# Two-block transformer on one core: local attention placed between tiles of the delta mixer's projection

## The chip, the cores and the metric

The kernel runs on one core of a Trainium2 chip (trn2). Its metric is the time of one launch in microseconds on the device; the median of three runs is given. One execution was also profiled. The core has TensorE (PE, matrix products), VectorE (DVE), ScalarE (ACT), GpSimd (POOL) and SyncE (SP), which here issues the weight loads. Each engine works through its own list of instructions in the order in which they are written; semaphores make one wait for another.

## The reference

Two blocks of two layers each run on 256 tokens of width 1024; the first block puts 16 meta tokens in front. All arithmetic is fp32. The change touches the first layer only. Its mixer projects the 272 normed tokens once and splits the result into a delta part and a window part:

```
proj = u @ w_in        # 272 x 1024 by 1024 x 2832
qa, ka, va, za, ba, aa, qb, kb, vb = split_cols(proj, AB_SIZES)
ya = delta_mixer(qa, ka, va, za, ba, aa, conv_w, a_log, dt_bias, a_out_g)
qb = rmsnorm(qb, bq_g) * (B_HD ** -0.5)      # 8 heads of 64
kb = rmsnorm(kb, bk_g)                       # 2 key heads of 64
yb = window_mixer(qb, kb, vb, sink)
return jnp.concatenate([ya, yb], axis=-1) @ w_out
```

- The delta mixer passes q, k and v (12 chunks of 128 channels) through a centred convolution of five taps over the tokens and a SiLU, divides q and k by their length for each of four heads of 128, and then solves and scans a gated delta rule in both directions.
- The window mixer is attention with |t - s| <= 128, a penalty on the distance with one slope for each head, a sink logit for each head, and the 16 meta tokens as keys without a penalty.

## The kernel before

**Layout.** Activations are kept transposed, channels on partitions and 272 tokens along the row. Every fp32 product with weights is made of three products of rounded parts: high by high, low by high and high by low. A block of 512 weight columns (2 MB) lands in one of the two halves of `raw`; for each quarter ACT writes the high part `w_hi` (L1140) and DVE the low part `w_lo` (L1615). A tile is 128 output columns: 8 x 3 matmuls of 128x272 at L524 into one of four banks. DVE then reads the bank, multiplies it by the token's norm factor (`scaled`, L1654) and so frees it for the tile after the next three.

**Order.** Weights are used in the order of `weight_plan`: four blocks `ab_qkvz` (16 tiles: q, k, v for the delta mixer, then z), one block `ab_qb` (four tiles, the window's queries), and `ab_kvb` (three tiles: its keys, its values, and the delta mixer's gates). All 23 tiles come first. In between DVE does a convolution after every second tile (`conv_after`: L1927 once, then L1929 four times), and ACT its SiLU (L1357).

**Head norms** (`head_norms`, `norm_steps`). For each unit ACT squares (L1187), PE sums over the partitions with a matrix of ones (L620), ACT takes the logarithm and the exponential that make the inverse root (L1197, L1200), and DVE scales (L1687, or L1970 for the delta heads). The window's five units run alone behind the projection.

**Window attention** (`attention`). It has 24 units: three groups of queries (16 meta tokens, twice 128) by eight heads. The loop's step k does parts of several units on each engine: PE the scores of unit k (L658), the three transposes of the probabilities of unit k-3 (L668) and the three value products of unit k-5 (L680); DVE the biased logits (L1766), their maximum (L1773, L1774), the sum with the sink and its inverse (L1784, L1785), the scaling of the probabilities (L1787) and the low part of a result (L1630); ACT the exponentials (L1235, L1236), the copy of the transposes (L1250) and the high part of a result (L1259). Every third step carries one of the eight delta head norms (`delta_norm`).

**Behind it.** `gated_delta` transposes k and v (L745), sums the decays (L753) and then works chunk by chunk; its first product is L770. The mask products of its inverse are POOL's (L2404). POOL's other work is the sum of squares for the norms (L2378) and some small loads.

## Time and profile before

| | |
|---|---|
| median of three runs | 1775.62 us (1772.45 to 1776.26) |
| the profiled execution: its own time | 1774.72 us |
| its span, first to last instruction | 1772.9 us |
| PE busy | 1669.5 us, 94% of the span |
| PE loading weights (beside its matmuls) | 1563.7 us |
| DVE busy | 1177.6 us, 66% |
| ACT busy | 816.9 us, 46% |
| POOL busy | 139.9 us, 8% |
| mean granted clock of PE | 0.939 |
| chain that ended last | PE 86%, DVE 9%, ACT 2%, issue 2% |

The granted clock is the share of PE's full speed that it was given in a stretch: 1.00 is 2.4 GHz, 0.50 is 1.2 GHz. A matmul's busy time runs from issue to its modelled end and overlaps the next one, so a busy PE need not be a PE at its full rate. The page's line of 40 slices shows where the clock was low; the stretches of the rows below do it in finer steps. The chain of waits is followed back from the last instruction: at each step to what released it.

### The profile page before, as it was taken

Reading aid. Unit: us, or ns where it says so; the run is one execution under the profiler, and the core shown is the slowest. Engines: PE = TensorE matmul, PEld = TensorE weight load, DVE = VectorE, ACT = ScalarE, POOL = GpSimd, SP = SyncE. Lnnn points to the kernel's source line nnn. Section 1 sums busy time; section 2 is a strip of 40 time slices with the busy share of each in tenths; the row PEclk is TensorE's granted clock in tenths of the full one; section 3 lists DMA queues with packets and bytes.
Section 4 is the critical chain, followed back from the end, with each engine's and each line's share of the span. In section 5 each row is a group of like instructions: output and inputs, shape, how many; then the busy total and the mean of one; then the engine's idle time right before and its main releaser. Section 6 shows DMA issues by size and latency. Waiting matters only on the chain.

```text
span 1772.9 us, 32025 instructions
## 1 busy us (share of the span) xinstructions
PE 1669.5 (94%) x12741; PEld 1563.7 (88%) x12741; DVE 1177.6 (66%) x2136; ACT 816.9 (46%) x1454; POOL 139.9 (8%) x142
## 2 busy tenths in 40 slices
PE   7979899899999889999999898999999999899998
PEld 6935688899999769999999587999998989799998
DVE  6865466577777566777766765666676666566766
ACT  4454322254345455444545445544453555554443
POOL 2000043010002101000200020100010001010000
PEclk9955699899999899999999689999999999999999
DMA  6410000145445304555454122455544444255552
GB/s 235 158 48 1 1 1 1 48 144 189 172 160 203 139 1 155 192 181 185 162 204 157 48 96 96 136 198 190 183 161 153 146 143 144 95 161 190 178 188 94
DMA packets 125816, 236.59 MB, mean 133 GB/s; under 512 B 2614, under 2 KB 50025, under 8 KB 125689
## 3 DMA queue, kind: packets, MB, share of 16 engines
q1 hardware_dynamic: 124393, 230.28, 37.5%
q0 software_dynamic: 1296, 4.53, 0.8%
q8 instruction: 90, 1.47, 0.3%
q14 instruction: 37, 0.30, 0.1%
HBM read 233.75 MB, written 1.05 MB: 132 GB/s over the span
## 4 chain that ended last, share of the span: by engine, by line
PE 86%; DVE 9%; ACT 2%; issue 2%; POOL 0%; SPq 0%; DMA 0%; DVEq 0%; ACTq 0%
PE ps L524 46%; PE ps L571 5%; PE ps L570 5%; PE ps L569 5%; PE ps L532 5%; PE ps L680 4%; PE ps L658 4%; DVE w_lo L1615 2%; PE ps L620 2%; PE ps L668 2%; PE ps L791 1%; PE ps L803 1%; PE ps L800 1%; DVE u_lo L1635 1%; DVE hidden L1666 1%
## 5 line engine op out<-in xcount | busy, mean ns | idle before, releaser
L1140 ACT ACTIVATE w_hi<-raw 128x1024 fp32r<-128x1024 f32 x440 | 460.1, 1051 | 301.0 <-PE ps L571 138.6
L1615 DVE TENSOR_TENSOR w_lo<-raw,w_hi 128x1024 fp32r<-128x1024 f32 x440 | 539.6, 1227 | 9.8 <-ACT w_hi L1140 9.6
L524 PE MATMUL ps<-u_hi,w_hi 128*128 128x256 f32 (+1 forms) x1544 | 444.5, 288 | 15.7 <-DVE u_lo L1635 8.7
L524 PE MATMUL ps<-u_hi,w_lo 128*128 128x256 f32 (+1 forms) x1544 | 440.5, 285 | 0.0
L524 PE MATMUL ps<-u_lo,w_hi 128*128 128x256 f32 (+1 forms) x1544 | 440.1, 285 | 0.0
L524 PEld LDWEIGHTS ps<-u_hi,w_hi 128*128 128x128 f32 x1544 | 294.4, 191 | 19.7 <-DVE u_lo L1635 10.8
L524 PEld LDWEIGHTS ps<-u_hi,w_lo 128*128 128x128 f32 x1544 | 294.6, 191 | 0.0
L524 PEld LDWEIGHTS ps<-u_lo,w_hi 128*128 128x128 f32 x1544 | 293.6, 190 | 0.3
L524 PE MATMUL ps<-a_hi,w_hi 128*128 128x256 f32 (+1 forms) x800 | 230.4, 288 | 5.3 <-DVE a_lo L1630 2.3
L524 PE MATMUL ps<-a_lo,w_hi 128*128 128x256 f32 (+1 forms) x800 | 227.7, 285 | 0.0
L524 PE MATMUL ps<-a_hi,w_lo 128*128 128x256 f32 (+1 forms) x800 | 227.5, 284 | 0.0
L569 PE MATMUL ps<-a_hi,w_hi 128*128 128x256 f32 (+1 forms) x688 | 195.1, 284 | 0.8 <-DVE hidden L1666 0.8
L571 PE MATMUL ps<-a_hi,w_lo 128*128 128x256 f32 (+1 forms) x688 | 195.6, 284 | 0.0
L570 PE MATMUL ps<-a_lo,w_hi 128*128 128x256 f32 (+1 forms) x688 | 195.3, 284 | 0.0
L1666 DVE TENSOR_TENSOR hidden<-ps,hidden 128x256 f32<-128x256 f32 (+1 forms) x272 | 116.0, 427 | 117.3 <-PE ps L571 60.2
L524 PEld LDWEIGHTS ps<-a_hi,w_hi 128*128 128x128 f32 x800 | 153.2, 192 | 7.2 <-DVE a_lo L1630 2.8
L1654 DVE TENSOR_TENSOR work<-ps,rs 128x256 f32<-128x256 f32 (+1 forms) x153 | 65.4, 428 | 141.6 <-PE ps L524 120.8
L524 PEld LDWEIGHTS ps<-a_hi,w_lo 128*128 128x128 f32 x800 | 153.6, 192 | 0.0
L524 PEld LDWEIGHTS ps<-a_lo,w_hi 128*128 128x128 f32 x800 | 152.5, 191 | 0.4
L569 PEld LDWEIGHTS ps<-a_hi,w_hi 128*128 128x128 f32 x688 | 129.8, 189 | 1.0 <-DVE w_lo L1615 1.0
L571 PEld LDWEIGHTS ps<-a_hi,w_lo 128*128 128x128 f32 x688 | 130.0, 189 | 0.0
L570 PEld LDWEIGHTS ps<-a_lo,w_hi 128*128 128x128 f32 x688 | 129.3, 188 | 0.0
(338 smaller groups left out, 2497.4 us busy)
## 6 DMA issues: line engine op xcount, KB each, us to landing
raw<-in_w_ff_dram SPq DMA_DIRECT2D x32, 2048.0 KB, 8.4
raw<-in_ffn_w_gu_dram SPq DMA_DIRECT2D x44, 1024.0 KB, 7.0
raw<-in_ffn_w_down_dram SPq DMA_DIRECT2D x10, 2048.0 KB, 7.8
raw<-in_xa_w_kv_dram SPq DMA_DIRECT2D x8, 2048.0 KB, 7.9
raw<-in_od_w_in_dram SPq DMA_DIRECT2D x6, 2048.0 KB, 8.0
raw<-in_w_in_ab_dram SPq DMA_DIRECT2D x5, 2048.0 KB, 8.5
raw<-in_ev_w_in_dram SPq DMA_DIRECT2D x5, 2048.0 KB, 7.8
raw<-in_xa_w_q_dram SPq DMA_DIRECT2D x4, 2048.0 KB, 7.8
```

What stands on the lines that cost most here:

```text
L524: mm = pe.matmul(bank[:, 0:n], wx[:, q, k * P:(k + 1) * P], x[ux][:, k, ts], start=k == 0 and i == 0, stop=k == KD - 1 and i == 2)
L532: mm = pe.matmul(bank[:, at:at + n_quarters * n].rearrange("p (q n) -> p q n", n=n), x[ux][:, k, ts], wx[:, q:q + n_quarters, k * P:k * P ...
L569: pe.matmul(tile_bank[t % 4][:, 0:n], hi[:, k, cols], a[0][:, at_k, ts], start=k == 0, stop=False)
L570: pe.matmul(tile_bank[t % 4][:, 0:n], hi[:, k, cols], a[1][:, at_k, ts], start=False, stop=False)
L571: mm = pe.matmul(tile_bank[t % 4][:, 0:n], lo[:, k, cols], a[0][:, at_k, ts], start=False, stop=k == chunks - 1)
L620: mm = pe.matmul(banks[u_ % 2][:, 0:n], matrix, hn_sq[:, u_ % 2, i * n:(i + 1) * n], start=i == 0, stop=i == tiles - 1)
L658: mm = pe.matmul((b4, b5)[v % 2][0:x["nq"], 0:x["nk"]], q, k, start=c == 0, stop=c == len(x["q"]) - 1)
L680: mm = pe.matmul(tile_bank[1 + v % 3][x["parts"], r * P:r * P + x["nq"]], vs[r], at_pt[0:rows, v % 2, c, 0:x["nq"]], start=c == 0, stop=c ...
L1140: act.activation(quarter(w_hi, b, q), raw_quarter(b, q), ACT.Copy).then_inc(high_split, 1)
L1615: dve.tensor_tensor(quarter(w_lo, b, q), raw_quarter(b, q), quarter(w_hi, b, q).bitcast(F32), ALU.subtract)\
L1654: dve.tensor_tensor(target, tile_bank[t][:, 0:n], rs[:, ts] if scale is None else scale, ALU.mult)\
L1666: dve.tensor_tensor(hidden[:, k, ts], tile_bank[t][:, 0:ts.stop - ts.start], hidden[:, k, ts], ALU.add)\
```

## The change

The window part is computed first, and the rest of the projection lies inside its attention loop.

- **Order of the blocks.** `ab_qb` and `ab_kvb` come before `ab_qkvz`. The five head norms of the window have the three tiles of `ab_kvb` and the first two of `ab_qkvz` between them. The other 14 tiles lie in steps 0 to 13 of the attention loop (`window_step`). A memset clears the quarter of `raw` that the second block does not fill.
- **Units.** The eight units of 16 queries become one of kind "meta": its 128 rows are 8 heads by 16 queries, taken from a copy `q_meta`, with a table for each row's slope and a sink for each row. So there are 17 units. These units have one bank for their transposes and one for their results (`turn_bank`, `attention_bank`), where there were two and three, since the projection holds the four tile banks.
- **Convolutions.** Chunks 2, 5, 8 and 11 stay on DVE, the other eight go to POOL with nine tensor_tensor operations each. ACT applies one Silu to all twelve chunks in step 12, after all convolutions.
- **Delta norms.** Two groups of four heads: one square of 128x1088, four sums into the tile banks, four logarithms, one exponential, one scaling. They lie in steps 13 to 15; the transposes of k and v in steps 16 to 18; the decays in steps 0 to 2.

Line numbers in the changed kernel are larger. 
```diff
-    add("ab_qkvz", [[cols(x, c)] for c in range(0, 2048, BLOCK)])
     add("ab_qb", [[cols(x, 2064)]])
     add("ab_kvb", [[cols(x, 2576, 256), cols(x, 2048, 128, into=256)]])
+    add("ab_qkvz", [[cols(x, c)] for c in range(0, 2048, BLOCK)])
...
+            if x["kind"] == "meta":
+                return b7[:, 0:n * NMETA].rearrange("p (c q) -> p c q", q=NMETA)
+            bank = b7 if near(x) else tile_bank[1 + v % 3]
+            return bank[x["parts"], 0:n * P].rearrange("p (c q) -> p c q", q=P)[:, :, 0:x["nq"]]
+        def near(x):
+            return x["kind"] in ("window", "meta")
+        def turn_bank(x, v):
+            return b6 if near(x) else (b6, b7)[v % 2]
...
-            for m in range(3):
+            for m in (1, 2):
                 for h in range(8):
                     yield m, h
+        WINDOW_UNITS, AB_BEFORE = 17, 2
+        CONV_DVE = (2, 5, 8, 11)
+        conv_part = area(mx, 9952, 2, T)
+        delta_sq, delta_r = area(work, 0, 4, T), area(work, 4 * T, 4, T)
...
         # TensorE, attention()
+                    if near(x):
+                        if v >= 1:
+                            pe.wait_ge(at_copied, v)
+                    elif v >= 2:
...
-            for t in range(3):
+            def kvb_tile(t):
                 split_ready(b, t if t < 2 else 3)
                 bank_free(b, t)
                 transposed_tile(t, u, full, tile_bank[t]).then_inc(tile_summed, 1 if t < 2 else 2)
+            def qkvz_tile(n):
+                tile_t(first_of("ab_qkvz") + n // 4, n % 4, u, full)
+            head_norms([(1, T, blk64)] * 5, between=lambda i: kvb_tile(i) if i < 3 else qkvz_tile(i - 3))
...
+            def window_step(k):
+                if k < 16 - AB_BEFORE:
+                    qkvz_tile(AB_BEFORE + k)
+                if k == 0:
+                    pe.wait_ge(M["ab_turn_read"], 1)
+                if k == 1:
+                    delta_decays()
+                if k == 2:
+                    pe.wait_ge(M["d_cum_read"], 1)
+                j = k - (16 - AB_BEFORE)
+                if j in (0, 1):
+                    if j == 0:
+                        pe.wait_ge(tile_read, tile_at[first_of("ab_out")])
+                    else:
+                        pe.wait_ge(M["d_rs"], 1)
+                    pe.wait_ge(M["d_sq"], j + 1)
+                    for h in range(A_HEADS):
+                        mm = pe.matmul(tile_bank[h][:, 0:T], ones, delta_sq[:, h], start=True, stop=True)
+                    mm.then_inc(M["d_qsum"], 1)
+                if j in (2, 3, 4):
+                    for i in (2 * j - 4, 2 * j - 3):
+                        delta_turn(i, *turn_list[i])
...
         # ScalarE
-            def conv(first_slot):
-                def silu(i, t):
-                    slot = first_slot + 4 * i + t
-                    if slot % 2 == 0 and slot >= 2:
-                        c = slot // 2 - 1
-                        act.wait_ge(M["conv_done"], c + 1)
-                        act.activation(qkv[:, c], qkv[:, c], ACT.Silu).then_inc(M["silu_done"], 1)
-                return silu
...
+            def window_step(k):
+                if k < 15:
+                    split_high(ab + 1 + (k + 1) // 4, (k + 1) % 4)
+                if k == 2:
+                    act.wait_ge(M["d_cum_read"], 1)
+                    act.activation(necc[0:NMETA, 0], gcc[0:NMETA, 0], ACT.Exp)
+                    act.activation(necc[:, 1:3], gcc[:, 1:3], ACT.Exp).then_inc(M["d_gate_exp"], 1)
+                j = k - (16 - AB_BEFORE)
+                if j == -2:
+                    act.wait_ge(M["conv_done"], 12)
+                    act.activation(qkv, qkv, ACT.Silu).then_inc(M["silu_done"], 1)
+                    log_and_exp()
+                if j == -1:
+                    act.wait_ge(M["silu_done"], 1)
+                    act.activation(delta_sq, qkv[:, 0:4], ACT.Square).then_inc(M["d_sq"], 1)
+                if j in (0, 1):
+                    act.wait_ge(M["d_qsum"], j + 1)
+                    if j == 1:
+                        act.wait_ge(M["d_normed"], 1)
+                    for h in range(A_HEADS):
+                        ins = act.activation(delta_r[:, h], tile_bank[h][:, 0:T], ACT.Ln, bias=eps)
+                    link(ins)
+                    act.activation(delta_r, delta_r, ACT.Exp, scale=-0.5).then_inc(M["d_rs"], 1)
+                    if j == 0:
+                        act.activation(delta_sq, qkv[:, 4:8], ACT.Square).then_inc(M["d_sq"], 1)
+                if j in (2, 3, 4):
+                    for i in (2 * j - 4, 2 * j - 3):
+                        m, source = turn_list[i]
+                        n = TILES[m][1] - TILES[m][0]
+                        act.wait_ge(M["d_turned"], i + 1)
+                        act.activation((v_tok if source == 8 else k_tok)[0:n, m], tile_bank[i % 4][0:n, 0:4 * P].rearrange(
+                            "p (h d) -> p h d", h=4), ACT.Copy).then_inc(M["d_copied"], 1)
...
         # VectorE
+                lag = 5 if near(units[0]) else 6
+                for k in range(n + lag):
                     if k < n:
                         maximum(k)
                     if 0 <= k - 1 < n:
                         normalise(k - 1)
-                    if k >= 6:
-                        result(k - 6)
                     if between is not None:
                         between(k)
+                    if k >= lag:
+                        result(k - lag)
+                    if after is not None:
+                        after(k)
...
+            def qkvz_step(c):
+                if c == 0:
+                    split_low(ab, 2)
+                scaled(za[:, c - 12] if c >= 12 else xa[:, c, 2:2 + T], c % 4, tile_at[ab] + c, full)
+                split_low(ab + 1 + c // 4, c % 4 - 1)
...
+            def conv_step(k):
+                if k + 1 in CONV_DVE:
+                    conv(k + 1)
...
+                j = k - (16 - AB_BEFORE)
+                if j in (0, 1):
+                    heads = qkv[:, 4 * j:4 * j + 4].rearrange("p h t -> p (h t)")
+                    dve.wait_ge(M["d_rs"], j + 1)
+                    dve.scalar_tensor_tensor(heads, heads, P ** -0.5 if j == 0 else 1.0, delta_r.rearrange("p h t -> p (h t)"),
+                                             ALU.mult, ALU.mult).then_inc(M["d_normed"], 1)
...
         # GpSimd
+            for c in range(12):
+                if c not in CONV_DVE:
+                    weights = [col("conv", 12 * j + c).to_broadcast([P, T]) for j in range(5)]
+                    taps = [xa[:, c, j:j + T] for j in range(5)]
+                    pool.wait_ge(tile_read, tile_at[phases["ab_qkvz"].first] + c + 1)
+                    pool.tensor_tensor(qkv[:, c], taps[0], weights[0], ALU.mult)
+                    link(pool.tensor_tensor(conv_part[:, 1], taps[1], weights[1], ALU.mult))
+                    for j in range(1, 5):
+                        if j < 4:
+                            pool.tensor_tensor(conv_part[:, (j + 1) % 2], taps[j + 1], weights[j + 1], ALU.mult)
+                        ins = pool.tensor_tensor(qkv[:, c], qkv[:, c], conv_part[:, j % 2], ALU.add)
+                        if j < 4:
+                            link(ins)
+                    ins.then_inc(M["conv_done"], 1)
```

DVE around one step of the window loop; `ps` is a bank, `att` the logits and probabilities, `mx` the projection and the convolutions. Before:

```order
L1766 SCALAR_TENSOR_TENSOR att<-early,ps 128x272 [waits at_exp,at_scored]
L1773 TENSOR_REDUCE small<-att 128x1 [waits dve_step]
L1774 TENSOR_SCALAR small<-small 128x1 [waits dve_step]
L1784 TENSOR_TENSOR small<-small 128x1 [waits at_exp]
L1785 RECIPROCAL small<-small 128x1 [waits dve_step]
L1787 TENSOR_SCALAR att<-att,small 128x272 [waits dve_step]
L1630 TENSOR_TENSOR a_lo<-ps,a_hi 64x128 [waits operand_high]
```

The same step in the changed kernel, one of the four that have a convolution on DVE:

```order
L1849 SCALAR_TENSOR_TENSOR att<-early,ps 128x272 [waits at_exp,at_scored]
L1856 TENSOR_REDUCE small<-att 128x1 [waits dve_step]
L1857 TENSOR_SCALAR small<-small 128x1 [waits dve_step]
L1867 TENSOR_TENSOR small<-small 128x1 [waits at_exp]
L1868 RECIPROCAL small<-small 128x1 [waits dve_step]
L1870 TENSOR_SCALAR att<-att,small 128x272 [waits dve_step]
L1737 TENSOR_TENSOR mx<-ps,rs 128x272 [waits tile_summed]
L1698 TENSOR_TENSOR w_lo<-raw,w_hi 128x1024 [waits high_split]
L1713 TENSOR_TENSOR a_lo<-ps,a_hi 64x128 [waits operand_high]
L2014 TENSOR_SCALAR mx<-mx,late 128x272 [waits tile_read]
L2016 SCALAR_TENSOR_TENSOR mx<-mx,late 128x272 [waits dve_step] x4
```

The tile's scaling, the weight split and the convolution have moved in between the scaling of the probabilities and the next unit's logits.

POOL, behind its small loads and ahead of the mask products. Before:

```order
L2383 DMA small<-in_a_log_dram 128x8
L2383 DMA small<-in_dt_bias_dram 128x8
L2383 DMA small<-in_b_sink_dram 128x8
L2383 DMA small<-in_od_w_g_2_dram 128x8x16
L2404 TENSOR_TENSOR work<-work,early 16x64 [waits d_nn]
```

In the changed kernel, the first convolution of eight alike:

```order
L2481 DMA small<-in_od_w_g_2_dram 128x8x16
L2502 TENSOR_TENSOR mx<-mx,late 128x272 [waits tile_read]
L2503 TENSOR_TENSOR mx<-mx,late 128x272
L2506 TENSOR_TENSOR mx<-mx,late 128x272 [waits pool_step]
L2507 TENSOR_TENSOR mx<-mx 128x272
L2506 TENSOR_TENSOR mx<-mx,late 128x272 [waits pool_step]
L2507 TENSOR_TENSOR mx<-mx 128x272
L2506 TENSOR_TENSOR mx<-mx,late 128x272 [waits pool_step]
L2507 TENSOR_TENSOR mx<-mx 128x272
L2507 TENSOR_TENSOR mx<-mx 128x272 [waits pool_step]
```

72 operations stand where there were none, each convolution behind a wait for its tile.

ACT where it does the SiLU of the convolutions, in the change at steps 12 and 13 of the loop; `w_hi` is a quarter of weights, `work` the squares. Before, at the end of the projection:

```order
L1140 ACTIVATE w_hi<-raw 128x1024 [waits tile_summed]
L1357 ACTIVATE mx<-mx 128x272 [waits conv_done]
L1140 ACTIVATE w_hi<-raw 128x1024 [waits tile_summed] x2
L1357 ACTIVATE mx<-mx 128x272 [waits conv_done]
L1339 ACT_TABLE_LOAD
```

In the changed kernel:

```order
L1309 ACTIVATE att,small<-att,small 128x272
L1213 ACTIVATE w_hi<-raw 128x1024 [waits tile_summed]
L1457 ACT_TABLE_LOAD
L1457 ACTIVATE mx<-mx 128x3264 [waits conv_done]
L1412 ACT_TABLE_LOAD
L1323 ACTIVATE att<-ps 16x128 [waits at_summed,at_turned]
L1323 ACTIVATE att<-ps 128x256
L1332 ACTIVATE a_hi<-ps 64x128 [waits at_summed]
L1308 ACTIVATE small<-small 128x1 [waits at_prob,at_turned,at_max]
L1309 ACTIVATE att,small<-att,small 128x272
L1213 ACTIVATE w_hi<-raw 128x1024 [waits tile_summed]
L1461 ACTIVATE work<-mx 128x1088 [waits silu_done]
```

Twelve Silu operations and their table load have moved from the projection into the loop as one, which waits for the last convolution; copies, results and exponentials of the next steps stand behind it.

## Rows read from the trace of the kernel before

**Rows 1.** Busy time by stretch; the first row names the columns.
```profile
core 0: us, PE busy (x) PEld busy (x) DVE busy (x) ACT busy (x) POOL busy (x), PEclk, DMA share, GB/s
22.30:92.60 70.30, 68.44 (x540) 67.87 (x538) 59.59 (x109) 30.10 (x38) 0.00 (x0) 1.00 0.49 162
113.00:196.20 83.20, 82.85 (x282) 44.62 (x281) 45.31 (x168) 40.93 (x165) 0.00 (x0) 0.50 0.00 1
147.24:183.26 36.02, 36.02 (x106) 18.66 (x106) 18.50 (x66) 16.98 (x63) 0.00 (x0) 0.50 0.00 1
1070.00:1080.00 10.00, 8.34 (x62) 7.90 (x62) 5.30 (x10) 5.53 (x10) 0.00 (x0) 1.00 0.57 197
```

**Rows 2.** Timeline of PE: start, length in us, instruction.
```profile
90.97 0.29 PE L524 MATMUL ps<-u_hi,w_lo 128*128 128x272 f32 x1
...
108.36 1.09 PE L658 MATMUL ps<-mx 64*16 64x272 f32 x4 [3.40 <-issue]
...
201.33 1.06 PE L770 MATMUL ps<-cst,small 16*128 16x16 f32 x8 [0.33 <-DVE small L1992]
```

**Rows 3.** Chain of waits, window attention: start, us, what.
```profile
178.00 1.66 PE ps L680 x6
...
180.87 0.74 PE ps L668 x3
181.60 1.66 PE ps L680 x6
183.26 1.21 PE ps L620 x2
```

**Rows 4.** Chain of waits, the other layer's attention, same columns.
```profile
645.57 1.05 PE ps L680 x6
...
647.41 1.05 PE ps L680 x6
```

**Rows 5.** Groups by line and shape, 112 to 200 us, columns as in the page.
```profile
L1787 DVE TENSOR_SCALAR att<-att,small 128x272 f32<-128x272 f32 x16 | 5.8, 361 | 0.6
...
L1197 ACT ACTIVATE work<-ps,cst 128x272 f32<-128x272 f32 x8 | 3.8, 474 | 0.1
...
L1774 DVE TENSOR_SCALAR small<-small 128x1 f32<-128x1 f32 x16 | 3.4, 214 | 0.6
...
L1784 DVE TENSOR_TENSOR small<-small 128x1 f32<-128x1 f32 x16 | 2.4, 151 | 1.7 <-ACT att L1236 1.7
```

**Rows 6.** The same view, 20 to 95 us.
```profile
L1615 DVE TENSOR_TENSOR w_lo<-raw,w_hi 128x1024 fp32r<-128x1024 f32 x24 | 29.2, 1217 | 0.0
...
L1140 ACT ACTIVATE w_hi<-raw 128x1024 fp32r<-128x1024 f32 x24 | 25.0, 1053 | 14.3 <-PE ps L524 14.1 <-DMA raw<-in_w_in_ab_dram 0.2
...
L1929 DVE SCALAR_TENSOR_TENSOR mx<-mx,late 128x272 f32<-128x272 f32 x46 | 23.1, 502 | 1.6
...
L1654 DVE TENSOR_TENSOR mx<-ps,rs 128x272 f32<-128x272 f32 x21 | 9.2, 438 | 3.9 <-PE ps L524 3.6 <-DVE mx L1918 0.3
...
L1927 DVE TENSOR_SCALAR mx<-mx,late 128x272 f32<-128x272 f32 x12 | 4.2, 353 | 0.0
...
L1357 ACT ACT_TABLE_LOAD x1 | 1.3, 1283 | 0.0
```

**Rows 7.** Timeline of POOL, delta mixer: start, length in us.
```profile
225.94 1.26 POOL L2404 TENSOR_TENSOR work<-early 128x512 f32<-128x512 f32 x1 [1.13 <-DVE mx L2031]
227.16 1.71 POOL L2404 TENSOR_TENSOR work<-work,early 128x512 f32<-128x512 f32 x1
```

**Rows 8.** Timeline of DVE, the same moments.
```profile
225.97 1.78 DVE L2022 TENSOR_TENSOR mx<-mx 128x512 f32<-128x512 f32 x1
227.67 1.23 DVE L2021 COPY small<-att 128x4 f32<-128x4 f32 x1
228.93 0.69 DVE L2022 TENSOR_TENSOR att<-att,mx 128x512 f32<-128x512 f32 x1
```

**Rows 9.** POOL's line L2378, whole trace: shortest, median, longest in ns.
```profile
L2378 POOL TENSOR_TENSOR square_sum<-square_sum,squares x77: 719/1192/1772, 11.0 to 1575.4; 128x256 f32<-128x256 f32 x56, 128x272 f32<-128x272 f32 x21
```

More of the change, by code:

```diff
@@ L991, in _ @@
+            attention(units, None, between=window_step)
             window_ready = op[0]
@@ L1751, in _, with attention @@
             at = [0]
-            def attention(units, between=None):
+            def attention(units, between=None, after=None):
                 base, n = at[0], len(units)
@@ L1891, in mlp_swiglu @@
                 down(b, ts, norm)
+            dve.memset(raw[:, 1, :, 3 * P:4 * P], 0.0)
             dve.wait_ge(turned, 1)
@@ L1973, in _ @@
[L1973 to L1977 removed]
+            link(dve.tensor_tensor(sink_of, table("meta_head"), sink, ALU.mult))
+            dve.tensor_reduce(sink_meta, sink_of, AX.X, ALU.add).then_inc(M["sink_meta"], 1)
```

234 lines of the change are left out of this document (116 added, 118 removed).

## Prediction, made before the changed kernel was run

> **What bounds the kernel now.** I read the stretches by time first, then PE's timeline at the stage borders, then the chain of waits, and only then the groups by line. From 22.3 to 92.6 us PE works through the first layer's input projection: 68.4 us busy out of 70.3, granted clock 1.00 [rows 1]. Its 540 matmuls in 70.3 us make 3.1 us for a tile of 24. The last projection matmul starts at 90.97 us, the first window score at 108.36 us [rows 2]: 17 us in which DVE and ACT work off the projection's tail and the five norms of the window's heads. From 113 to 196.2 us PE is busy 82.85 of 83.2 us, but at granted clock 0.50 [rows 1]. So the window attention is bound by PE at 1.2 GHz: one unit of 128 queries takes 181.60 - 178.00 = 3.60 us, and every third one carries a norm sum of 1.21 us [rows 3]. A unit of much the same work in the other layer, at the full clock, takes 647.41 - 645.57 = 1.84 us [rows 4]. The delta mixer's own algebra begins at 201.33 us [rows 2]. All the change's work lies before that point; what comes behind it (1772.9 - 201.3 = 1571.6 us) keeps its instructions. I therefore work out one number: when L770's first matmul starts in the changed kernel.
>
> **Up to step 0.** The projection now begins with the window's five blocks' worth: nine tiles (four of qb, three of kvb, two of qkvz) stand ahead of the attention instead of 23, and the five head norms lie between them. 91.3 less 14 tiles of 3.1 us is 47.9 us; five sums at half of 1.21 us add 3.0; six small transposes, the doubling of the keys and the new copy of the meta queries (ACT, a few operations of some 0.4 us) end at about 54 us. That is step 0 of the attention. The 17 us gap is gone, because PE has tiles while ACT and DVE do the norms. The 24 units become 17: the eight with 16 queries go, one "meta" unit comes.
>
> **One step of the new loop.** Steps 0 to 11 each hold an attention unit and a tile; the last convolution must be done in step 12, since ACT then waits for all twelve before its one Silu. Per step:
> - PE: 1.84 + 3.1 = 4.9 us at the full clock.
> - ACT: 16.98 us for nine units [rows 1] is 1.9, with the old delta norms in it, plus 1.05 for a quarter of weights [rows 6]: 2.9 us. Never the bound here.
> - DVE: 18.50 us for nine units is 2.06, less a third of the old norm scaling, an operation like L1654's 0.44: 1.9. To this come the split w_lo 1.22, the scaled tile 0.44, and one convolution in three steps, (0.353 + 4 x 0.502) / 3 = 0.79 [rows 6]. Together 4.4 us, just under PE.
> - POOL: eight convolutions of nine operations of 128x272. The nearest row has 719 ns as its shortest [rows 9]; a following one starts 0.04 us before that (1.26 long, 1.22 apart) [rows 7], so 0.68 x 72 = 49 us, or 4.1 us a step.
>
> By these figures alone PE would set the step at 4.9 us. But DVE and POOL do not run beside each other freely. POOL works from 225.94 to 227.16 and DVE's L2022, which reads two SBUF operands and starts at 225.97, takes 1.78 us; the same operation with POOL quiet takes 0.69 [rows 7, 8]. POOL's next then takes 1.71 instead of 1.26, and behind it a DVE copy of four columns takes 1.23. They take turns, each waiting for the other's whole instruction. The Trainium skill ("SBUF — State Buffer", section "SBUF: two separate sides") says the same as a rule that speaks against this change: the port pair that the two share is locked for a whole instruction, by DVE operations with two SBUF inputs or in a two-port mode, and the loser blocks. By this rule the step is the sum of both engines' locked time, without it 4.9 us; the trace agrees with the rule.
>
> What DVE locks per step: w_lo 1.22, convolution 0.79, the probabilities' scaling 0.36, and the two tiny ones 0.21 and 0.15 [rows 5, 6] (the four-column copy waited too, so I count them): 2.7 us. The score bias, tile scaling and result split read PSUM and one SBUF operand; I count them free. 4.1 + 2.7 = 6.8 us. **I take 6.8 us a step.** Lower end: no turn-taking at all, 4.9 us. Upper end: each of the 5.7 locking instructions of a step waits a whole POOL operation, 4.4 + 5.7 x 0.68 = 8.2 us. If DVE ran ahead of POOL, ACT would wait for POOL in step 12 instead, so the sum stays.
>
> PE is then busy 4.9 of 6.8 us, 72%. A stretch of tiles mixed with head norms with 83% busy keeps clock 1.00 (the last row) [rows 1]; a dense attention of this kind keeps 0.50. I assume some cold spells, hidden in PE's 1.9 us of slack.
>
> **Behind step 12.** The tail has few tiles and much latency. From ACT's step 12: attention part 1.5, split 1.05, two table loads of 1.28 and a Silu of 3264 columns, three times L1140's 1.05: 8.3 us. Step 13: 2.5 and a square of 1.1. Step 14: PE's four norm sums, cold 4 x 1.21 = 4.8 us, four logarithms of 0.47 and an exponential of 1.1, the second square 1.1: 8.9. Step 15: sums 4.8, logarithms and exponential 3.0: 7.8. By then 28.6 us. Step 16 waits for this, then two turns of four transposes at 0.25 us each (three took 0.74) [rows 3] and copies: 3.5. Steps 17 and 18: transposes and values 2.4, turns 2, waiting for copies: 4.8 each. Steps 19 to 21 (transposes, values, twelve small matmuls of the meta unit, each behind the copy and the split of the one before, because there is now one bank for turns and one for results): 2.4, 1.7, 2.3. Sum 48 us; all warm some 42, with more waits 54. The decays, their cumulative sums and the transposes of k and v, which came behind the attention before, are in it or hidden in steps 0 to 2. The wait added on ACT in step 12 has the copies, results and exponentials of steps 13 on queued behind it, and with these PE's scores; that is why the steps are counted in series.
>
> **Sum.** L770 starts at 54 + 12 x 6.8 + 48 = 183.6 us instead of 201.3: 17.7 us less. The profiled execution took 1774.72 us, span 1772.9, which stands 0.9 below the median of 1775.62. 1774.7 - 17.7 = 1757.0, against the median 1758.
>
> What else is priced at nothing: the first weights (the same 2 MB block), the memset of raw on DVE (the quarter it clears belongs to the second block, which PE reads long after), the small table loads on POOL's queue, which stand ahead of its convolutions as before; the delta mask operations behind them start only after 183 us, POOL being free by about 136.
>
> **Rivals.**
> - *A, the forecast*: DVE and POOL take turns, 6.8 us a step: 1758. Chance 0.48.
> - *B, PE bound*: the turn-taking costs little, because POOL lags in harmless gaps. 54 + 12 x 4.9 + 48 = 160.8, 40.5 us less: 1735. For it: DVE's many PSUM operations, in which POOL can work. Against it: what DVE and POOL did to each other [rows 7, 8]. Chance 0.22.
> - *C, every lock waits in full*: 7.8 to 8.2 us a step, L770 at 195.6 to 200.4: 1770 to 1775. For it: POOL has always an operation queued, so the next begins the moment DVE lets go; POOL's mean under load is well above its shortest. Chance 0.18.
> - *D, slower*: the clock. If PE falls to 1.2 GHz as in the old window stage and stays, a step is 3.60 + 6.2 = 9.8 us: 54 + 117.6 + 48 = 219.6, 18.3 us more: 1794. It decides from (201.3 - 102) / 12 = 8.3 us a step, i.e. if PE is cold for about 70% of the loop. For it: PE stayed at 0.50 for 83 us while busy 99.6%. Against it: each step has 24 dense matmuls of the kind that kept 1.00. Chance 0.10. The Trainium skill ("TensorE: Matmul & The Clock Gate", "Part 4: PE-mode transpose") says that transposes don't count as activity in the way matmuls do, which would leave the attention's part weaker still; the other layer's units with their three transposes each held the full clock [rows 4], so the trace bears it out at most in part.
> - *E, it doesn't do what it says*: weights, misc loads or the meta unit's inputs are late and the loop starts late, about 0 to 5 us less than before: 1772. Chance 0.02.
>
> **How the numbers follow.** Time 1758. The range takes in A, B and the better part of C: 1734 to 1773. Changes under 0.2% (3.6 us) can't be told from none here. Faster: A, B and three quarters of C, 0.84; same: the rest of C and part of E, 0.06; slower: D, 0.10.
>
> **What would show it.** After the change: PE's granted clock near 1.00 from 54 to 135 us; DVE's w_lo at a mean of 1.5 to 1.9 us instead of 1.22 in this stretch, and the convolutions' scalar_tensor_tensor near 1.1 instead of 0.50; POOL's 128x272 operations over 0.8 us; step distance of the scores 6.8 us; the first score near 53; the Silu on ACT at about 138; L770 at 184. Wrong it is if DVE's durations stay as they are (B), if the step is 8 us or more (C, D), or if ACT's tail is not in the chain.

## The result, and the profile after

The changed kernel takes 1744.06 us (median of four runs, 1737.77 to 1746.24), beside 1774.03 for the kernel before (median of four, 1770.53 to 1776.26). The ratio is 0.9827 with a 95% interval of 0.9801 to 0.9854: some 30 us less, where 17.7 were forecast. The profiled execution took 1741.96 us, span 1739.6, so 33.3 us less than the span before. PE is busy 1633.7 us (94%), DVE 1158.7 (67%), POOL 202.2 (12%); PE's mean granted clock is 0.962 instead of 0.939.

In the changed kernel the tile's matmuls are L546, scores L685, transposes L698, values L724; `w_lo` is L1698, the tile's scaling L1737, the result's low part L1713; DVE's convolutions are L2014 and L2016, POOL's L2502 to L2507; the first delta product is L796. In some experiments an edit shifts these lines by two (L798, L726, L1851).

The first view is the timeline of PE in the changed kernel: start, length in us, instruction, and in brackets the idle time before it with what ended it.

```profile
68.29 0.72 PE L685 MATMUL ps<-mx 64*128 64x272 f32 x2 [2.14 <-DVE small L2076]
...
81.78 0.29 PE L546 MATMUL ps<-u_lo,w_hi 128*128 128x272 f32 x1
...
83.25 0.72 PE L685 MATMUL ps<-mx 64*128 64x272 f32 x2
83.91 0.49 PE L698 MATMUL ps<-cst,att 128*16 128x128 f32 x3
87.19 1.70 PE L724 MATMUL ps<-att,mx 16*64 16x128 f32 x6 [2.79 <-DVE a_lo L1713]
94.22 0.72 PE L685 MATMUL ps<-mx 64*128 64x272 f32 x2
...
137.10 2.10 PE L1034 MATMUL ps<-work,cst 128*128 128x272 f32 x8 [0.90 <-DVE mx L1737]
139.13 0.72 PE L685 MATMUL ps<-mx 64*128 64x272 f32 x2
...
165.33 1.03 PE L796 MATMUL ps<-cst,small 16*128 16x16 f32 x4
```

The first score starts at 53.31 us and the delta mixer's algebra at 165.33, where it was 201.33 [rows 2]: 36.0 us earlier. The sixteen scores of 128 queries start at 53.31, 57.18, 62.21, 68.29, 73.91, 78.01, 83.25, 94.22, 99.46, 104.70, 110.64, 115.88, 121.12, 128.88, 134.12 and 139.13. The first twelve steps take 67.8 us, 5.65 each. Six of the fifteen steps are exactly 5.24, which is PE's own work at the full clock (the first experiment shows it). The first five have less to do, because the transposes and values of the units lag behind the scores: in the first experiment, where PE never waits, they take 3.87 to 5.03. Two steps are long: 10.97 (from the seventh score) and 7.76 (from the thirteenth). A smaller stop lies early: the fourth score waits 2.14 us for DVE's copy of the decays (L2076), and the step behind it takes 5.62.

The same kernel by stretch, columns as in [rows 1]:

```profile
57.00:121.00 64.00, 58.41 (x369) 48.72 (x368) 56.60 (x120) 25.33 (x72) 57.50 (x67) 0.92 0.25 88
...
85.00:90.00 5.00, 2.81 (x11) 2.18 (x12) 4.86 (x12) 1.86 (x5) 4.84 (x6) 0.69 0.01 3
90.00:95.00 5.00, 5.00 (x25) 4.49 (x24) 0.79 (x3) 1.58 (x4) 4.77 (x7) 0.62 0.00 0
...
52.40:121.25 68.85, 63.26 (x400) 52.77 (x400) 61.35 (x132) 28.25 (x84) 62.19 (x72) 0.93 0.26 92
...
165.30:1739.60 1574.30, 1496.16 (x11830) 1438.36 (x11829) 1048.97 (x1809) 718.04 (x1194) 130.48 (x125) 0.96 0.40 138
```

In the loop PE, DVE and POOL are each busy nine tenths of the time: three engines of nearly equal load. The clock is 0.92 there, against 0.50 in the window stage before [rows 1]. The first two short stretches are the long step: PE idles, the clock falls, and the next tile runs at half speed (from 88.89 to 94.29, 5.4 us instead of 3.2). The last row is all that follows the delta mixer's start; it was 1571.6 us long before.

Groups by line and shape in the changed kernel, 57 to 121 us, to be held against [rows 5, 6]:

```profile
L2507 POOL TENSOR_TENSOR mx<-mx 128x272 f32<-128x272 f32 x31 | 31.1, 1003 | 0.6
...
L2506 POOL TENSOR_TENSOR mx<-mx,late 128x272 f32<-128x272 f32 x22 | 16.3, 740 | 1.7
L1698 DVE TENSOR_TENSOR w_lo<-raw,w_hi 128x1024 fp32r<-128x1024 f32 x11 | 14.8, 1349 | 0.0
L2016 DVE SCALAR_TENSOR_TENSOR mx<-mx,late 128x272 f32<-128x272 f32 x16 | 13.3, 829 | 0.6
...
L1870 DVE TENSOR_SCALAR att<-att,small 128x272 f32<-128x272 f32 x11 | 5.9, 536 | 0.4
...
L2014 DVE TENSOR_SCALAR mx<-mx,late 128x272 f32<-128x272 f32 x4 | 2.6, 653 | 0.0
L1857 DVE TENSOR_SCALAR small<-small 128x1 f32<-128x1 f32 x11 | 2.4, 214 | 0.4
L1867 DVE TENSOR_TENSOR small<-small 128x1 f32<-128x1 f32 x11 | 2.2, 201 | 0.0
```

`w_lo` costs 1.35 us instead of 1.22, the convolution's four operations 0.83 instead of 0.50, the probabilities' scaling 0.54 instead of 0.36, L2014 0.65 instead of 0.35, L1867 0.20 instead of 0.15; L1857 never waited (214 ns in both). Over a step that is 0.13 + (0.30 + 4 x 0.33) / 3 + 0.18 + 0.05 = 0.90 us.

### The profile page after: what moved, and what is told of

It is laid out like the page before. It is cut to its first block, busy times and chain, and to the rows that moved or that the text cites. A ratio compares the mean times of both kernels' runs of the same rounds, so it can differ in the third digit from the quotient of the medians.

```text
span 1739.6 us, 31776 instructions
## 1 busy us (share of the span) xinstructions
PE 1633.7 (94%) x12684; PEld 1552.0 (89%) x12684; DVE 1158.7 (67%) x2044; ACT 804.9 (46%) x1391; POOL 202.2 (12%) x214
## 3 DMA queue, kind: packets, MB, share of 16 engines
HBM read 233.76 MB, written 1.05 MB: 135 GB/s over the span
## 4 chain that ended last, share of the span: by engine, by line
PE 83%; DVE 11%; issue 3%; ACT 2%; POOL 0%; SPq 0%; DMA 0%; DVEq 0%; ACTq 0%
PE ps L546 45%; PE ps L593 6%; PE ps L592 6%; PE ps L591 6%; PE ps L554 5%; DVE w_lo L1698 3%; PE ps L724 3%; PE ps L685 2%; PE ps L642 2%; PE ps L817 1%; PE ps L829 1%; PE ps L826 1%; PE ps L698 1%; DVE u_lo L1718 1%; DVE hidden L1749 1%
## 5 line engine op out<-in xcount | busy, mean ns | idle before, releaser
L1698 DVE TENSOR_TENSOR w_lo<-raw,w_hi 128x1024 fp32r<-128x1024 f32 x440 | 540.5, 1229 | 11.2 <-ACT w_hi L1213 10.9
L546 PE MATMUL ps<-u_hi,w_hi 128*128 128x256 f32 (+1 forms) x1544 | 448.0, 290 | 15.4 <-DVE u_lo L1718 9.0
L546 PE MATMUL ps<-u_hi,w_lo 128*128 128x256 f32 (+1 forms) x1544 | 442.0, 286 | 0.0
L546 PE MATMUL ps<-u_lo,w_hi 128*128 128x256 f32 (+1 forms) x1544 | 441.8, 286 | 0.0
L546 PEld LDWEIGHTS ps<-u_hi,w_hi 128*128 128x128 f32 x1544 | 296.0, 192 | 22.1 <-DVE u_lo L1718 11.0
L546 PEld LDWEIGHTS ps<-u_hi,w_lo 128*128 128x128 f32 x1544 | 296.1, 192 | 0.0
L546 PEld LDWEIGHTS ps<-u_lo,w_hi 128*128 128x128 f32 x1544 | 294.9, 191 | 0.5
L546 PE MATMUL ps<-a_hi,w_hi 128*128 128x256 f32 (+1 forms) x800 | 230.3, 288 | 5.3 <-DVE a_lo L1713 2.3
L546 PE MATMUL ps<-a_lo,w_hi 128*128 128x256 f32 (+1 forms) x800 | 227.7, 285 | 0.0
L546 PE MATMUL ps<-a_hi,w_lo 128*128 128x256 f32 (+1 forms) x800 | 227.4, 284 | 0.0
L546 PEld LDWEIGHTS ps<-a_hi,w_hi 128*128 128x128 f32 x800 | 153.2, 192 | 7.2 <-DVE a_lo L1713 2.8
L1737 DVE TENSOR_TENSOR work<-ps,rs 128x256 f32<-128x256 f32 (+1 forms) x153 | 65.4, 427 | 139.6 <-PE ps L546 118.8
L546 PEld LDWEIGHTS ps<-a_hi,w_lo 128*128 128x128 f32 x800 | 153.6, 192 | 0.0
L546 PEld LDWEIGHTS ps<-a_lo,w_hi 128*128 128x128 f32 x800 | 152.5, 191 | 0.4
L2473 POOL COPY square_sum<-squares 128x256 f32<-128x256 f32 (+1 forms) x11 | 5.7, 516 | 1112.9 <-ACT squares L1235 1092.3
```

The source lines that it names most:

```text
L546: mm = pe.matmul(bank[:, 0:n], wx[:, q, k * P:(k + 1) * P], x[ux][:, k, ts], start=k == 0 and i == 0, stop=k == KD - 1 and i == 2)
L1698: dve.tensor_tensor(quarter(w_lo, b, q), raw_quarter(b, q), quarter(w_hi, b, q).bitcast(F32), ALU.subtract)\
L1737: dve.tensor_tensor(target, tile_bank[t][:, 0:n], rs[:, ts] if scale is None else scale, ALU.mult)\
```

## Experiments

All ratios are to the kernel before, run on the same chip at the same time. The place to look at is the start of the first delta product, "delta start" below; the whole time scatters more (the changed kernel run again shows by how much).

### One operation of each POOL convolution

```diff
+ins = pool.tensor_tensor(qkv[:, c], taps[0], weights[0], ALU.mult)
-pool.tensor_tensor(qkv[:, c], taps[0], weights[0], ALU.mult)
-link(pool.tensor_tensor(conv_part[:, 1], taps[1], weights[1], ALU.mult))
-...   # the three further products and four sums
```

> The changed kernel, but each of the eight convolutions on POOL is only its first of nine operations (the rest of these convolutions is left out). Theory 1, as the trace of the changed kernel suggests: POOL's operations slow DVE's by about 0.8 us a step, DVE and PE are then level at 5.2 us, and the loop's excess over 12 x 5.24 us (4.9 us) comes from steps in which DVE is late. Without POOL's work DVE has 4.4 us a step, so PE sets 5.2 in every step: the first L796-like matmul comes 5 us earlier, about 160, w_lo back at 1.22 us. Theory 2, the forecast's: turn-taking sets the step in full: 8 us or more earlier. Rival: POOL is beside the path, no change within 1 us.

Measured: 1729.43 us, ratio 0.974 (0.9703 to 0.9778), delta start 154.52. Its groups and its row for 57 to 121 us:

```profile
L1698 DVE TENSOR_TENSOR w_lo<-raw,w_hi 128x1024 fp32r<-128x1024 f32 x14 | 17.0, 1216 | 0.0
...
L2016 DVE SCALAR_TENSOR_TENSOR mx<-mx,late 128x272 f32<-128x272 f32 x16 | 8.0, 502 | 0.6
```

```profile
57.00:121.00 64.00, 64.00 (x437) 52.76 (x436) 54.28 (x143) 33.58 (x84) 10.85 (x7) 1.00 0.36 129
```

With POOL nearly quiet (one operation in nine is left) DVE's durations are those of [rows 6] again, PE is never idle, and every step from the sixth score to the fifteenth takes 5.24 us. DVE is busy 25.53 us in the six of these steps from 80.81 to 112.25 us, 4.3 us a step, where the prediction had 4.4. So POOL's work, mostly through DVE, costs 10.8 us of delta start in all. That includes the two long steps and the early stop, which are gone too: without the sharing DVE keeps up. My first theory expected 5 us, the forecast's 8 or more; the size falls on the forecast's side, but not for its reason. The first twelve steps are 10.15 us shorter, and all of it lies at three places where PE stopped or ran cold: 3.7 us at the early stop, 5.7 at the long step and 0.7 at the step of 5.94.

### All convolutions on DVE

```diff
-CONV_DVE = (2, 5, 8, 11)
+CONV_DVE = tuple(range(12))    # and chunk 0 in step 0
```

> All twelve convolutions on DVE, none on POOL. If the turn-taking costs little (0.8 us a step), moving eight convolutions to POOL is worth more than it costs: DVE has 3.6 + 2.36 = 6.0 us a step in steps with a convolution, loop 71 us instead of 68, kernel 3 to 5 us slower than the changed one. If turn-taking cost what the forecast said (2.4 us a step), this kernel would be faster than the changed one by 5 us or more.

Measured: 1741.9 us, ratio 0.9816 (0.9783 to 0.9849), delta start 168.21, 2.9 us later than in the changed kernel, about as expected (3 to 5), while the whole time can't be told from it. PE of this kernel at the long step:

```profile
86.32 0.72 PE L685 MATMUL ps<-mx 64*128 64x272 f32 x2
86.97 0.49 PE L698 MATMUL ps<-cst,att 128*16 128x128 f32 x3
90.97 1.70 PE L724 MATMUL ps<-att,mx 16*64 16x128 f32 x6 [3.50 <-DVE a_lo L1713]
```

The long step (11.3 us) is there with an idle POOL. What makes it is DVE's load, whether by the sharing or by more convolutions; the shared port alone does not explain it. Eight convolutions on POOL thus save DVE 8 x 2.36 = 18.9 us (0.354 + 4 x 0.502 each) and give some 11 us of that back in longer operations (0.90 us in twelve steps).

### The tiles ahead of the attention

```diff
 def window_step(k):        # PE; ACT's split_high and DVE's qkvz_step, conv likewise
-    if k < 16 - AB_BEFORE:
-        qkvz_tile(AB_BEFORE + k)
...
+for n in range(2, 16):     # between the head norms and the attention
+    qkvz_tile(n)
```

> The changed kernel with its 14 tiles, their splits and the DVE convolutions ahead of the attention loop instead of in it; the 17 units, POOL's convolutions and the grouped delta norms stay. If the gain is the clock and the overlap: the attention runs at 1.2 GHz again with 3.6 us a unit, scores start near 97, delta algebra near 190 to 195, 25 to 28 us later than in the changed kernel, i.e. nearly all of the gain is gone (1770). Rival: the gain is mostly the seven units less and the grouping of norms: then this kernel keeps more than half of the 30 us (1757 or less).

Measured: 1750.26 us, ratio 0.988 (0.9839 to 0.9921), delta start 179.25. The first score and the clock came as expected (96.27 us for 97, units of 3.6 us), the delta start did not (179.25 for 190 to 195): the rival was right, over half the gain stays without the interleaving. The chain of waits of this kernel in its attention (start, us, what):

```profile
109.94 1.27 PE ps L685 x2
111.21 0.74 PE ps L698 x3
111.94 1.66 PE ps L724 x6
113.61 1.20 PE ps L685 x2
```

Its units take 113.61 - 109.94 = 3.67 us, cold as before [rows 3]. So the interleaving itself is worth 179.25 - 165.33 = 13.9 us of delta start. Its first score stands at 96.27 us, where the kernel before has 108.36: 12.1 us come from what stood between the last tile and the first score. These are the head norms, which now lie between tiles, and ahead of them the last SiLU and a table load, which held ACT until its first square at 97.94 us in the kernel before. The two were not separated.

### Eight units of 16 queries again instead of the meta unit

```diff
-for m in (1, 2):
+for m in (1, 2, 0):        # and no unit of kind "meta"
     for h in range(8):
         yield m, h
```

> The changed kernel with the eight units of 16 queries in place of the one meta unit, behind the 16 units of 128 (24 units in all, one result bank). If these units cost what they did before (2.2 us each where PE set their pace), seven more are 14 us at the end of the loop, where nothing hides them: delta algebra near 179, time near 1758. Rival: they fill the idle time of PE in the tail and cost less than 5 us.

Measured: 1747.51 us, ratio 0.9864 (0.9838 to 0.989), delta start 175.06: 9.7 us later than in the changed kernel, between the 14 expected and the rival's 5. PE of this kernel in the added units:

```profile
165.30 0.41 PE L698 MATMUL ps<-cst,att 16*16 16x16 f32 x3
165.64 0.93 PE L724 MATMUL ps<-att,mx 16*64 16x16 f32 x6
167.06 0.40 PE L698 MATMUL ps<-cst,att 16*16 16x16 f32 x3 [0.49 <-ACT att L1319]
167.39 0.92 PE L724 MATMUL ps<-att,mx 16*64 16x16 f32 x6
168.80 0.40 PE L698 MATMUL ps<-cst,att 16*16 16x16 f32 x3 [0.49 <-ACT att L1319]
```

A small unit costs 1.7 us here, and each one's transposes wait 0.49 us for ACT's copy of the last ones; that this is latency, because one bank for turns and one for results let little overlap, is my reading and was not tested. The three parts add up: 13.9 (interleaving) + 12.1 (norms and SiLU off the path) + 9.7 (meta unit) = 35.7, of 36.0 measured. They are one each against different neighbours, so the sum is a cross-check and no proof. The four-head delta norms were not tried alone.

### Two results in flight

The values of unit i waited until DVE had split the result of unit i-1, though only the meta unit writes all of the bank. The values of two neighbouring units can stand in it together:

```diff
-if i >= 1:
+if x["kind"] == "meta":
     pe.wait_ge(operand_split, split0 + i)
+elif i >= 2:
+    pe.wait_ge(operand_split, split0 + i - 1)
```

> The value products of a unit wait for the split of the result two units back instead of one (units of even and odd heads write different halves of the bank's partitions); only the meta unit waits for the last. If the single result bank is what makes PE wait (7.8 us in five waits, one of 2.8 us followed by a cold spell), the loop's excess goes: delta algebra 5 to 8 us earlier, 1738. Rival: DVE is the bound of the loop and the wait only moves to the scores: within 1 us.

Measured: 1730.39 us, ratio 0.9758 (0.9723 to 0.9794), delta start 158.56. PE of this kernel where the changed one stood still, and in step 14; then its row for 57 to 121 us:

```profile
83.48 0.72 PE L685 MATMUL ps<-mx 64*128 64x272 f32 x2
84.14 0.50 PE L698 MATMUL ps<-cst,att 128*16 128x128 f32 x3
84.56 1.01 PE L726 MATMUL ps<-att,mx 16*64 16x128 f32 x6
88.72 0.72 PE L685 MATMUL ps<-mx 64*128 64x272 f32 x2
...
128.69 0.80 PE L698 MATMUL ps<-cst,att 128*16 128x128 f32 x3 [2.57 <-ACT att L1325]
...
131.48 3.71 PE L1036 MATMUL ps<-work,cst 128*128 128x272 f32 x8 [0.33 <-ACT work L1463]
```

```profile
57.00:121.00 64.00, 61.86 (x410) 51.07 (x410) 61.43 (x129) 27.82 (x79) 59.01 (x67) 0.97 0.26 90
```

Every step from the sixth score to the fifteenth takes 5.24 us; both long steps are gone, DVE's operations being as long as before (`w_lo` 1.39 us on average). The early stop of 2.14 us is still there. A new one of 9.73 us appears at steps 14 to 15: PE waits 2.57 us for ACT, which is in its Silu (2.93 us) between two table loads of 1.28, and the norm sums then run cold at 3.71 and 3.96 us instead of 2.1.

### The result's split first in DVE's order

```diff
+if k >= lag:
+    result(k - lag)
 if between is not None:    # the tile's scaling, w_lo
     between(k)
-if k >= lag:
-    result(k - lag)
```

> The changed kernel, with one edit on DVE in the attention loop: the low part of a result (a_lo) stands ahead of the tile's scaling and the weight split instead of behind them. The wait of TensorE's value products for one result bank stays. Theory (the stall between steps 6 and 7 comes because the result split stands behind 1.8 us of DVE work): the wait of 2.79 us shrinks to about 1 us, steps 6 to 7 and 12 to 13 lose 2 to 5 us together, first delta product at 160 to 163 instead of 165.3. Rival (DVE's order matters less than the bank: DVE now waits for ScalarE's high part with the tile's scaling and the split queued behind it, so that TensorE's next tile is late): first delta product at 166 or later, DVE idle before a_lo, and steps over 5.24 us throughout.

Measured: 1740.06 us, the median of four launches of which one took 5406.77 us and the others 1736.52 to 1743.38; ratio 0.9814 (0.9774 to 0.9854), delta start 166.18, at the rival's 166. At the long step:

```profile
82.58 0.72 PE L685 MATMUL ps<-mx 64*128 64x272 f32 x2
83.23 0.50 PE L698 MATMUL ps<-cst,att 128*16 128x128 f32 x3
86.32 1.70 PE L724 MATMUL ps<-att,mx 16*64 16x128 f32 x6 [2.59 <-DVE a_lo L1713]
```

My expectation of a wait of 1 us fell. The split does come 1.7 us earlier in DVE's own step (2.09 us after its L1849, at 83.81 and 85.90; in the changed kernel 3.80, at 82.97 and 86.77), but the wait is 2.59 instead of 2.79 us and the step 10.4. DVE simply runs that much further behind PE before the bank stops PE. The rival's second half, steps over 5.24 us throughout, is not seen either. The second long step does go (5.66 us from the thirteenth score), but the step behind the Silu takes 8.73 instead of 5.01. For the first long step, what matters is how far DVE may lag, not where in its step the split stands.

### Both, and the two results again

> The same DVE order together with two result banks (value products of unit i wait for the split of unit i-2). If the second bank already takes the whole wait off the path, nothing is left for the order to give: first delta product within 1 us of the 158.6 of the kernel with two results alone. If DVE's wait for ScalarE starves the tiles, it is 2 us or more later.

Measured with both edits: 1734.92 us, ratio 0.9797 (0.9762 to 0.9832), delta start 163.34. That is 4.8 us behind the 158.56 of the first kernel with two results, where "within 1 us" was expected, and 2.7 behind the 160.62 measured for it beside this run (below). The step from the fourth to the fifth score takes 7.07 us here. It follows the early stop:

```profile
69.77 1.27 PE L685 MATMUL ps<-mx 64*128 64x272 f32 x2 [2.14 <-DVE small L2078]
```

The same wait of 2.14 us stands in six of the other traces, and the step behind it takes 5.62 us in the changed kernel (clock 0.70 from 68.29 to 74.00), 4.11 in the result-first kernel and in the run below (1.00 in the same stretch), and 7.07 here (0.61).

> The kernel with two results again, beside the two others on one chip. The first time its first delta product stood at 158.56 us and its time was 0.9758 of the kernel before. The theory that its gain is built into the order expects the delta product within 0.5 us of that, a stall at steps 14 to 15 of 9 to 10 us, and a ratio of 0.973 to 0.979; the rival that it was a chance of this run expects a stall in the loop's steps 6 to 7 or 12 to 13 to come back.

Measured for two results again, on the same chip: 1732.45 us, ratio 0.9779 (0.975 to 0.9807), delta start 160.62. No long step in the loop: from the sixth score to the fifteenth all are 5.24 us. The delta start lies 2.1 us later than the first time, against 0.5 expected: 1.0 from the first score (54.59 instead of 53.55), 1.7 from the step behind the Silu (11.47 instead of 9.73), and 0.7 off elsewhere, where the step behind the early stop took 4.11 instead of 5.62. So the gain is built into the order and the last step's size is not. The result first gives nothing on top. Its 2.7 us loss could be read as the tiles starved by DVE's wait, the expectation's second case; but the step behind the early stop alone is 2.96 us longer in it (7.07 against 4.11), at equal waits. It is of the size of the scatter.

### Six convolutions on each engine, and ten on POOL

Both with two results in flight:

```diff
-CONV_DVE = (2, 5, 8, 11)
+CONV_DVE = (1, 3, 5, 7, 9, 11)
```

> With the two result halves, and the convolutions six on DVE and six on POOL instead of four and eight. If PE sets the loop at 5.24 us a step and DVE has room (measured 4.4 us of own work and 0.9 of waiting for POOL), two more convolutions on DVE (0.4 us a step) and fewer waits for POOL (0.2 us less) leave the step at 5.24: within 1 us of the two-halves kernel, delta algebra near 158.6. Rival: DVE is at its limit (5.2 us), so the step goes to 5.5 and the kernel is 3 us slower.

Measured: 1737.14 us, ratio 0.9803 (0.9773 to 0.9832), delta start 162.85. Delta start is 2.2 to 4.3 us behind the two runs with four convolutions on DVE, so the expected 1 us was missed; but the rival's steps of 5.5 us are not there either, from the sixth score to the fourteenth all take 5.24. Two early steps take 6.8 and 6.9 us: DVE has a convolution in every second step there and the decays besides.

```diff
-CONV_DVE = (2, 5, 8, 11)
+CONV_DVE = (5, 11)
```

> With the two result halves, and ten convolutions on POOL, two on DVE. The forecast's rule, by which the locked times of both engines add up: POOL 90 operations of 0.64 us is 58 us, DVE's w_lo, convolutions and scalings about 20 us, together 78 us from 52 us on, so that ACT waits for the last convolution in step 12 until 130 us instead of 122.5, and the delta algebra is 7 to 8 us later than in the two-halves kernel. Rival: the times overlap in good part, POOL is done by 124 us, and the kernel is within 2 us.

Measured: 1738.28 us, ratio 0.9819 (0.9789 to 0.9849), delta start 167.64. ACT of this kernel:

```profile
116.98 1.28 ACT L1459 ACT_TABLE_LOAD   x1
132.87 2.92 ACT L1459 ACTIVATE mx<-mx 128x3264 f32<-128x3264 f32 x1 [14.61 <-POOL mx L2509]
```

The loop is at PE's rate (PE busy all of 57 to 121 us, clock 1.00, and the early stop gone with DVE's convolution of chunk 2, behind which the decays' copy stood) and then ACT waits 14.6 us for POOL's last convolution. POOL's total decides from here, and with it the one Silu for all twelve chunks.

Here the forecast's rule came out better than its rival. It expected POOL's end and the Silu at 130 us and a delta start 7 to 8 us later; the Silu starts at 132.87, and the delta start is 9.1 us behind the first kernel with two results and 7.0 behind the second. The rival, POOL done by 124 us, fell. POOL's 90 operations take from 53.47 to 132.83 us, 79.4 in all. With DVE idle a convolution of nine takes it 6.4 us (from 126.47 to 132.83), so ten would be 64: some 16 us are waiting, two thirds of the 24 us in which DVE works at `w_lo`, scalings and its two convolutions (12 x 1.58 + 2 x 2.36). Where POOL is the bound, its waits for DVE do lengthen the path.

By delta start eight to four is the best of the three splits tried with two results; the intervals of the ratios overlap. POOL ends at 121.25 us in the changed kernel, 7 us before the Silu starts at 128.22.

### The changed kernel again

> The changed kernel once more, on the same chip as the others of this call: ratio 0.983 to the kernel before as measured first. The two stalls of its loop (steps 6 to 7 and 12 to 13, 5.7 and 2.5 us over 5.24) should be there again if they are built into the order (a convolution on DVE in front of a result's split, one result bank), and be elsewhere if they were chance.

Measured: 1746.07 us, ratio 0.984 (0.9808 to 0.9873); profiled span 1733.2, delta start 165.39, long steps of 11.02 and 7.74 us at the same places. Up to there the two executions agree within 0.1 us. Behind it they don't: 1567.8 us here, 1574.3 in the first, with the same instructions.

## Why the prediction was right, and where it was not

The mechanism was right in its place and its direction: PE leaves the slow clock, the gap closes, and POOL and DVE hold each other up. The size of the last was wrong, and that the time lies in the range of 1734 to 1773 us is owed to its width, which took in the rival B. Of the signs that the forecast named, the first score came (53.31 us for 53). The others were missed in size: `w_lo` at 1.35 us instead of 1.5 to 1.9, the convolution's operations at 0.83 instead of 1.1, POOL's at 0.74 and 1.00 around the 0.8, steps of 5.65 us instead of 6.8, the clock at 0.93 instead of near 1.00, the Silu at 128.2 instead of 138, the delta product at 165.3 instead of 184.

**What bounded, and where the gain lies.** Right: the cold window stage and the 17 us gap before it were the place, and all of the gain stands ahead of the delta start. Behind it 1571.6 us before stand beside 1574.3 and 1567.8 after; the difference between two executions of one kernel is larger than either step, so no give-back is shown.

**Up to step 0.** Forecast 54, measured 53.31.

**PE's part of a step.** Forecast 4.9, measured 5.24: scores 0.67, transposes 0.43, values 0.94, tile 3.2. DVE's own 4.4 was right (4.3 in the first experiment). The granted clock stayed high, as forecast against rival D: 0.93 in the loop.

**DVE and POOL: the term that was mis-sized.** The prediction added POOL's 4.1 us a step and DVE's locked 2.7 us to 6.8. Twelve steps took 67.8 us, 5.65 each; the eleven without the long one average 5.17. Where PE never waits (first experiment) the same twelve take 57.7 us. By the sum, 72 operations and twelve steps of locks make 81.6 us; POOL's 72 operations lay within 68.85 us, its waits for tiles included. Here the step is near the largest of three nearly equal loads and not their sum, and DVE's operations grew by 0.9 us a step instead of costing the step 1.9. Two stretches show why, in the timelines of POOL and of DVE in the changed kernel:

```profile
80.19 0.83 POOL L2503 TENSOR_TENSOR mx<-mx,late 128x272 f32<-128x272 f32 x1
81.10 0.72 POOL L2506 TENSOR_TENSOR mx<-mx,late 128x272 f32<-128x272 f32 x1
...
104.99 1.55 POOL L2502 TENSOR_TENSOR mx<-mx,late 128x272 f32<-128x272 f32 x1 [2.46 <-DVE mx L1737]
106.50 0.63 POOL L2503 TENSOR_TENSOR mx<-mx,late 128x272 f32<-128x272 f32 x1
```

```profile
79.76 3.29 DVE L2016 SCALAR_TENSOR_TENSOR mx<-mx,late 128x272 f32<-128x272 f32 x4
...
104.83 1.21 DVE L1698 TENSOR_TENSOR w_lo<-raw,w_hi 128x1024 fp32r<-128x1024 f32 x1
```

At 104.83 `w_lo` starts first and keeps its 1.21 us, as the prediction had it; POOL's operation waits and takes 1.55 instead of 0.63. Here POOL pays, and POOL had time: its mean grew from 0.64 or 0.76 (with DVE idle, in the kernel with ten convolutions on POOL) to 0.74 and 1.00 us (L2506, L2507), with no one waiting for it. At 79.76 each engine has a convolution: DVE's operations take 0.82 us instead of 0.50, POOL's 0.72 and 0.83 instead of 0.64. In strict turns each would need 0.50 + 0.64 = 1.14. They overlap in part. The Trainium skill ("SBUF — State Buffer", section "Who interferes with whom") says that whoever issues first holds the shared pair for the whole instruction and the other is blocked; the stretch at 104.83 agrees, the one at 79.76 does not, and the measurement decides. So [rows 7, 8] were read rightly for one form of instruction and then charged to all, the tiny ones (L1857 never waited) included, and charged to the step instead of to the engine that had slack.

**What the prediction missed.** PE's values wait for DVE through the one result bank. DVE at 61.35 / 12 = 5.1 us a step is level with PE; a lag of 2.8 us becomes a stop of PE, and the stop costs 10.97 - 5.24 = 5.7 us because the clock falls with it. The prediction priced one bank in the tail only. Two results in flight take both long steps away at unchanged DVE durations. Moving the split leaves the first one. That shows the bank as what turns DVE's lag into a stop; the lag itself is DVE's load, by the first two experiments.

The decays were put down as hidden in steps 0 to 2, at no cost. They were not: the wait for DVE's copy of them makes the step to the fourth score 6.08 us instead of the 3.87 of the first experiment, and the next one, with the clock down, 5.62 instead of 4.11. That is 3.7 us, and two results in flight do not take it away.

**The tail.** Forecast 48 us, measured 44.2 (from the thirteenth score at 121.12 to 165.33). The Silu was counted by three of L1140's 1.05, 3.15 us, and took 2.93; it started at 128.2 instead of 138, the loop being shorter. The norm sums were warm: 2.10 us instead of the 4.8 assumed; where they were cold, with two results in flight, they took 3.7 and 4.0.

**The sum.** Start 53.3 + loop 67.8 + tail 44.2 = 165.3, forecast 54 + 81.6 + 48 = 183.6. Of the 18.3 us, 13.8 are the loop's, 3.8 the tail's and 0.7 the start's. The time lies between the forecast A (6.8 us a step) and B (4.9, 1735), nearer to B. C and D are excluded by the steps of 5.24 us and the clock, E by the first score.

**The best kernel.** Two results in flight, with eight convolutions on POOL: 0.9758 (0.9723 to 0.9794) and 0.9779 (0.975 to 0.9807). It and the changed kernel were not run side by side on one chip, so they are compared through the kernel before: the ratios' intervals overlap (0.9827, 0.9801 to 0.9854), and the delta starts (158.6 and 160.6 against 165.3 and 165.4) lie apart.

## What to carry to other kernels

Where two engines share a port, ask for each form of instruction which of the two pays, and whether that one has slack; add the waits to that engine's own load, and take the largest load, not the sum. For the engine that bounds, as POOL did with ten convolutions, each wait lengthens the path. When three engines are within a few per cent of each other, look for the buffer that ties them: how far may the slower one lag before it stops the other. A stop of TensorE is priced with the cold stretch behind it, here between once and two and a half times the wait itself.

## What the runs showed of the hardware

- One wait of 2.79 us on PE cost 5.7 us of the step: the granted clock was 0.69 and 0.62 in the two stretches of 5 us around and behind it, and a tile took 5.4 us instead of 3.2.
- What a stop costs behind itself varies at equal waits: after one of 2.14 us the next step took 4.11, 5.62 or 7.07 us in different kernels, at granted clock 1.00, 0.70 and 0.61 from 68.29 to 74.00 us.
- Attention units between dense tiles ran at clock 1.00 (first experiment) whose like alone ran at 0.50 for 83 us while PE was never idle [rows 1].
- POOL does a 128x272 fp32 product of SBUF operands in 0.63 to 0.64 us when DVE is quiet (the kernel with ten convolutions on POOL, 126.47 to 127.71 us).
- A Silu over 3264 columns takes 2.93 us on ACT and ties all twelve chunks to the last convolution (14.6 us of waiting with ten of them on POOL).
- Two executions of one kernel agreed within 0.1 us over the first 165 us and differed by 6.5 us over the rest.
